# Sparse decode attention: sample by sample with positions on partitions, instead of all samples at once with heads on partitions

## What is computed

```python
_, sel = lax.top_k(sc, n_sel)                       # 256 of 2049 positions
rows_past = cache_kv[phys, pidx % PAGE_SIZE]        # keys and values, 2 kv heads x 64
s = jnp.einsum('bqcgd,bqncd->bqcgn', qg, k_sel).astype(jnp.float32) * DSA_SCALE
bias = rel_bias[t5_bucket(q_pos[None, :, None] - sel)]
s = jnp.where(valid[:, :, None, None, :], s + bias.astype(jnp.float32), -jnp.inf)
p = jax.nn.softmax(s, axis=-1)
o = jnp.einsum('bqcgn,bqncd->bqcgd', p, v_sel.astype(jnp.float32))
```

## Time and profile before

| | us |
|---|---|
| median of three runs (lowest, highest) | 1309.33 (1307.5, 1312.77) |
| the profiled execution | 1306.96 |
| its span, from the first instruction to the last | 1305.2 |
| TensorE busy in the span | 1190.2 (91%) |
| VectorE busy | 674.9 (52%) |
| ScalarE busy | 396.8 (30%) |
| GpSimd busy | 91.3 (7%) |
| end of the last `expand` (MLA decode) | 673.5 |
| first matmul of the output projection | 814.96 |

### The profile page before, as it was taken

The page is one execution under the profiler, slowest core; times in us unless marked ns, Lnnn a source line. Parts: engine busy times, 40 slices in busy tenths (PEclk is TensorE's granted clock), DMA queues, the critical chain, the costliest instruction groups (busy, mean ns, idle before and its releaser), DMA issues.

```text
span 1305.2 us, 22152 instructions
## 1 busy us (share of the span) xinstructions
PE 1190.2 (91%) x8993; PEld 1035.9 (79%) x8993; DVE 674.9 (52%) x1449; ACT 396.8 (30%) x766; POOL 91.3 (7%) x135
## 2 busy tenths in 40 slices
PE   6699999978999999999979966976999999979997
PEld 4588885444878999999865345966999999979997
DVE  1635835638897877777651031527333344276330
ACT  3322324523676555555542311012010100100001
POOL 2000002002035000001000010000000000000000
PEclk9799999979999999999987978987999999989999
DMA  9587631022011021113216634221333333332321
GB/s 324 151 268 196 191 114 41 3 70 90 2 74 74 1 74 74 74 74 138 76 65 219 241 141 197 72 58 33 97 88 88 96 89 88 86 89 75 99 72 65
DMA packets 138529, 135.96 MB, mean 104 GB/s; under 512 B 18222, under 2 KB 132283, under 8 KB 135668
## 3 DMA queue, kind: packets, MB, share of 16 engines
q1 hardware_dynamic: 133668, 83.29, 22.0%
q0 software_dynamic: 4784, 51.60, 10.4%
HBM read 131.40 MB, written 3.47 MB: 103 GB/s over the span
## 4 chain that ended last, share of the span: by engine, by line
PE 78%; DVE 11%; DMA 5%; ACT 3%; issue 2%; SPq 1%; POOL 0%; DVEq 0%; ACTq 0%
PE psV L1118 22%; PE psV L943 13%; PE psA L1118 10%; PE psA L686 6%; PE psV L1058 3%; PE psV L880 2%; PE psV L904 2%; PE psA L923 2%; PE psV L642 2%; DMA wide<-cache_kv,rows_of 2%; PE psA L1050 2%; PE psV L748 2%; PE psA L980 2%; PE psV L1089 1%; DVE wide_r L2062 1%
## 5 line engine op out<-in xcount | busy, mean ns | idle before, releaser
L943 PE MATMUL psV<-r_r,wide_r 128*128 128x260 f32 x1536 | 206.4, 288 | 3.6 <-DVE msk L1887 3.2
L943 PEld LDWEIGHTS psV<-r_r,wide_r 128*128 128x128 f32 x1536 | 190.1, 189 | 5.5 <-issue 2.9
L1118 PE MATMUL psV<-qiz_r,wring_r 128*128 128x260 f32 x688 | 124.0, 284 | 0.0
L1409 ACT ACTIVATE wring<-psV 128x512 f32<-128x512 f32 x128 | 76.3, 598 | 86.1 <-PE psV L943 69.7
L1118 PEld LDWEIGHTS psV<-qiz_r,wring_r 128*128 128x128 f32 x688 | 100.5, 190 | 0.0
L1888 DVE TENSOR_REDUCE msk<-wring 128x8 f32<-128x512 f32 x128 | 86.5, 676 | 0.0
L686 PE MATMUL psA<-wide_r,wring_r 128*128 128x260 f32 x432 | 79.7, 289 | 6.6 <-DVE hT_r L2097 6.6
L2051 DVE TENSOR_TENSOR wide<-wide,psV 128x520 f32 (+1 forms) x22 | 15.3, 696 | 134.7 <-PE psV L1118 134.7
L1118 PE MATMUL psA<-qiz_r,r_r 128*128 128x260 f32 x352 | 71.8, 286 | 14.1 <-DVE hT_r L2005 14.1
L1118 PE MATMUL psA<-hT_r,r_r 128*128 128x260 f32 x352 | 71.9, 286 | 0.0
L1118 PE MATMUL psA<-qiz_r,wring_r 128*128 128x260 f32 x352 | 71.4, 285 | 0.0
(11 more groups left out here) (464 smaller groups left out, 2483.3 us busy)
## 6 DMA issues: line engine op xcount, KB each, us to landing
wring<-w_ffn_in SPq DMA_DIRECT2D x44, 512.0 KB, 3.7
wide<-w_ada SPq DMA_DIRECT2D x11, 1024.0 KB, 6.9
wring<-w_ffn_out SPq DMA_DIRECT2D x16, 704.0 KB, 4.7
tok<-w_ada SPq DMA_DIRECT2D x9, 1024.0 KB, 8.1
wring<-w_in SPq DMA_DIRECT2D x24, 256.0 KB, 3.4
wring<-w_out SPq DMA_DIRECT2D x8, 512.0 KB, 4.4
wring<-w_in SPq DMA_DIRECT2D x20, 128.0 KB, 2.7
hT<-x_prompt SPq DMA_DIRECT2D x4, 512.0 KB
```

What stands on the lines that cost most here:

```text
L943: mm = pe.matmul(kx[m % 2][:, hf, :], w, wtab[:, b % 2, l, 2 * k + hf, :], start=(k == 0 and w is high and l == 0), stop=(k == 1 and w is ...
L1118: mm = pe.matmul(out[:, hf, 0:HT], w[:, k, :], x[:, hf * HT:(hf + 1) * HT], start=(k0 + k == 0 and x is xh and w is high), stop=(k0 + k == ...
L1409: A(sq2[m % 2].rearrange("p (x n) -> p x n", x=2), kx[m % 2][:, :, 0:256], ACT.Square).then_inc(kx_squared, 1)
```

## The change

The sparse decode is written like the MLA decode, with positions on partitions, one sample after the other. `k_product` now writes the scores of one sample (`dps`, 128 positions x 17 slots x 8 heads) with the transposed keys as weights and the sample's 8 queries as moving data. `sparse_scores` adds the bias and the mask (`bmd`), and `shift`, `exps`, `row_sums`, `normalise`, `head_max` and `head_sum` serve the sparse samples as b = 8 to 15. `weigh_values(b)` uses the value half of the same buffer, so each sample is fetched once. The mask stays on the chip (`maskx`); its HBM round trip, the 64-row softmax and its transposes, `qdz` and `ptb` are gone. The bias table `far` is made once, during the prompt attention (`far_table`), and `bmd` per sample by GpSimd (`mask_bias`), two samples ahead. The `latent_out` matmuls of group A are done sample by sample within the MLA decode. The first output weights are loaded when the mask is ready, and the prompt's part of the projection input is split apart from the samples' part (`split_prompt`). In part, with "..." where lines are left out:

```diff
+            def far_table():
...
+                for j in range(NPG + 1):
+                    cols = ohf[:, j:PAST:NPG] if j < NPG else ohf[:, PAST:PAST + 1].broadcast_to([NBUCK, 128])
+                    mm = pe.matmul(farps[:, j * 8:(j + 1) * 8], cols, rb64[:, 0:8], start=True, stop=True, skip_group_check=True)
+                mm.then_inc(far_full, 1)
...
+                if u == 8:
+                    far_table()
...
+                if j == 10 and b >= 1:
+                    pe.wait_ge(lat_out, b)
+                    mm = latent_out(b - 1)
...
+                for x in range(4):
+                    j = c4 * 4 + x
+                    mm = pe.matmul(dps[:, j * 8:(j + 1) * 8], kdT[:, c4 % 2, x * 128:(x + 1) * 128], qd[:, b * 8:(b + 1) * 8],
+                                   start=True, stop=True, skip_group_check=True)
...
+            def weigh_values(b):
+
+                pe.wait_ge(pm_ready, NB + b + 1)
+                pe.wait_ge(lat_out, NB + b)
+                for j in range(NPG + 1):
+                    rows = kvp[b % 3][:, j, 128:256] if j < NPG else tok[:, 4, 416:544]
+                    q = 32 * (j % 4)
+                    mm = pe.matmul(latd[q:q + 32], pm32[b % 2][:, j, :], rows, start=(j < 4), stop=(j > NPG - 4), skip_group_check=True)
+                mm.then_inc(lat_pv, 1)
...
+            for b in range(NB):
+                weigh_values(b)
+                if b >= 1:
+                    values_out(b - 1)
+                if b + 2 < NB:
+                    k_scores(b + 2)
...
+            for b in range(NB):
+                if b >= 1:
+                    exps(NB + b)
+                for c4 in range(4 if b + 1 < NB else 0):
+                    if b == 0 and c4 == 2:
+                        exps(NB)
+                    take_keys(4 * b + 4 + c4)
+                take(NB + b)
...
+            for b in range(NB):
+                sparse_scores(b)
+                for step in (shift, row_sums, normalise):
+                    step(NB + b)
...
+            def mask_bias(b):
+                if b == 0:
+                    g.wait_ge(far_taken, 1)
+                    g.wait_ge(mask_ready, 1)
+                if b >= 2:
+                    g.wait_ge(d_taken, b - 1)
+                g.tensor_tensor(bmd[:, b % 2].rearrange("p (j h) -> p j h", h=8), far,
+                                maskx[:, b, :].unsqueeze(2).broadcast_to([128, NPG + 1, 8]), ALU.add).then_inc(bm_ready, 1)
...
+                if b == NB - 3:
+                    for x in range(2):
+                        mask_bias(x)
...
-            for b in range(2, NB):
-                if b >= 3:
-                    g.wait_ge(a_full, A_KD + 4 * b - 8)
-                kv_rows_of(b, b % 3)
...
+            for b in range(NB):
+                head_max(NB + b)
+                if b + 2 < NB:
+                    g.wait_ge(lat_pv, NB + b)
+                    kv_rows_of(b + 2, (b + 2) % 3)
+                head_sum(NB + b)
+                if b + 2 < NB:
+                    mask_bias(b + 2)
```

More of the change, by code:

```diff
@@ L950, in expand, with latent_out @@
                     mm = pe.matmul(last_total[:, 8:16], earlier, ends[:, 8:16], start=True, stop=True, skip_group_check=True)
-                mm.then_inc(kx_full, 1)
+                elif m % 4 == 2 and KA + m // 4 == STEPS + 1:
+                    pe.wait_ge(top_done, 1)
+                    mm = pe.matmul(newm, maskx[:, :, NPG], ident[:, 127:128], start=True, stop=True, skip_group_check=True)
+                if j == 10 and b >= 1:
+                    pe.wait_ge(lat_out, b)
+                    mm = latent_out(b - 1)
+                mm.then_inc(kx_full, 1)
+            def latent_out(b):
+                for k in range(2):
+                    mm = pe.matmul(olps[:, k * 8:(k + 1) * 8], olr[b % 2][:, k * 128:(k + 1) * 128], sel[:, 64:72], start=True, stop=True,
+                                   skip_group_check=True)
+                return mm
             def rope_turn(b):
@@ new lines, in k_product, with k_scores @@
+                if c4 == 3:
+                    mm = pe.matmul(dps[0:NB, 128:136], kT[:, SEQ:T], qd[:, b * 8:(b + 1) * 8], start=True, stop=True, skip_group_check=True)
+                    mm.then_inc(d_full, 1)
+            def k_scores(b):
+                for c4 in range(5):
+                    if c4 < 4:
+                        k_turn(b, c4)
+                    if c4 >= 1:
+                        k_product(b, c4 - 1)
+            def weigh_values(b):
[6 more added lines that the diff above has]
+                mm.then_inc(lat_pv, 1)
@@ new lines, in values_out @@
+            def values_out(b):
+                pe.wait_ge(lat_out, NB + b + 1)
+                mm = pe.matmul(odps[:, b * 8:(b + 1) * 8], olr[b % 2][:, 0:128], sel[:, 64:72], start=True, stop=True, skip_group_check=True)
+                if b == NB - 1:
+                    mm.then_inc(od_full, 1)
+            k_scores(0)
+            weigh(NB - 1)
+            k_scores(1)
+            pe.wait_ge(lat_out, NB)
+            latent_out(NB - 1).then_inc(ol_full, 1)
+            for b in range(NB):
[5 more added lines that the diff above has]
+                if b == 0:
+                    pe.wait_ge(ol_taken, 1)
+                    pe.wait_ge(v_free, V_OV - 1)
+                    for h in range(H):
+                        for k in range(2):
+                            mm = pe.matmul(sv(V_OV)[(h % 2) * 64:(h % 2) * 64 + 64, 0, (h // 2) * 8:(h // 2) * 8 + 8],
+                                           wukv[:, k, h * 128 + 64:(h + 1) * 128], olT[:, k, :].rearrange("p (b h) -> p h b", b=NB)[:, h, :],
+                                           start=(k == 0), stop=(k == 1), skip_group_check=True)
+                    mm.then_inc(v_full, 1)
@@ L1100, in pe_tail @@
+            values_out(NB - 1)
         def pe_tail(pe):
```

270 lines of the change are left out of this document (91 added, 179 removed).

## The result

The changed kernel took 1359.1 us (median of 4 runs, 1342.21 to 1362.61) beside 1311.05 us for the kernel before on the same chip: ratio 1.0326, 95% interval 1.0228 to 1.0425. It is 48 us slower, where 28 was forecast. The time lies inside the range, the direction is right, and the mechanism in the sparse decode is the one that was named. But the largest part of the loss arises elsewhere, in the prompt attention. The ratio is one of means, and leaves out the longest run of the changed kernel (1362.61, counted as slow), which is the profiled one; so ratios are taken from the runs, and shares from the traces. Its span is 1360.5 us, 55.3 more than before.

A forecast was written before the change was run, and what follows sets the result against it. TensorE was taken to bound the kernel outside the sparse decode, GpSimd's switches the new sparse decode. There +21.4 us, with +6.4 from small terms before it: +27.8 on 1309.33 gives 1337 us, range 1300 to 1362.

The forecast's parts named there:

- The switches: Sparse decode: GpSimd passing from reduction to TENSOR_TENSOR and back, 10 and 8.5 us, a pair per sample, period 21.1 us.
- the +21.4 of the forecast: Sparse decode: the output projection would start at 836.4 us instead of 815.0, before the shift from earlier terms.
- The direction that had no row of its own: GpSimd's switch from TENSOR_TENSOR back to the reduction: bounded by 0 and 33 us, taken at 8.5.
- The slowing by a fetch: Sparse decode: the first switch of a pair runs beside a fetch, so it was taken at 10 us, not 8.5.
- Both rivals with cheap switches: GpSimd's switches at 6 us each, 1298 us, chance 0.11; or costing nothing that counts, 1256 us, chance 0.05.
- The free period of 8.4 us: Sparse decode without switch costs: 8.4 us per sample, set by the fetch; TensorE's own sum was 7.6.
- The rival with free switches: GpSimd's bare ISA rows cost nothing that counts: 8.4 us per sample, total 1256 us; chance 0.05.
- pairs of 21 to 24.6: Rival in the sparse decode: fetches slow GpSimd's switches still more, total 1355 to 1375 us; slower than forecast had chance 0.14.
- the signs that were named: Profile after: GpSimd gaps of 8 to 12 us, reductions 21 us apart, TensorE waits, clock 0.5 to 0.7, projection near 843.
- The far table: Prompt attention: `far_table` adds 34 TensorE instructions of 0.112 us, 3.8 us in all, bounds 2.7 and 7.6.
- `latent_out`: MLA decode: 28 added TensorE instructions, 3.1 us.
- The switches around `mask_bias(0)` and `(1)`: End of MLA decode: this GpSimd pair needs some 19 us and just fits; up to 4 us more if slowed.

The follow-up runs named there:

- e4: Changed kernel with the fetch of sample b + 2 issued by GpSimd behind mask_bias(b + 2), not between head_max and head_sum: 1351.79 us, one run.
- e1: Changed kernel with mask_bias issued by VectorE and no longer by GpSimd: 1309.41 us.
- e3: Kernel before plus 17 unread matmuls at attention step 8, weights 32 x 128 (every 16th column), 8 moving columns: 1339.31 us, ratio 1.0208.
- e7: Kernel before plus the burst of e3, but with 128 adjacent weight columns per matmul and not every 16th: 1332.77 us, ratio 1.0166.
- e2: Changed kernel with the far table's 17 matmuls issued one per attention step, 8 to 24, and copied at step 26, not 10: 1341.15 us.
- e5: Changed kernel with the edits of e1 and e2, and adjacent weight columns for the far table: 1292.11 us, ratio 0.9864.
- e9: Changed kernel with mask_bias on VectorE, and the far table in one burst with adjacent columns in the sparse decode: 1284.96 us, ratio 0.9817.

## Why the prediction was right, and where it was not

**The switches.** Right in place, cause and nearly in size. Forecast 18.5 us for a pair (10 and 8.5) and a period of 21.1; measured 9.8 to 11.2 plus 5.8 to 6.0, and 19.4. Five periods are 97.1 us where 105.5 were forecast, which is about the difference between the +21.4 of the forecast and the +13.2 measured there. The direction that had no row of its own, back to the reduction, was taken at 8.5 and is 5.9. The slowing by a fetch, taken at 1.5, is 3.5 to 4, on a base of 7.0 and not 8.5 (e4): that the sum of 10 came out near 10.8 is two errors that nearly cancel. e1 shows that the switches set the period: without them it is 12.96 us. Both rivals with cheap switches fall, since a pair is 16 to 17 us. The Trainium skill's figure, about 6 us (GPSIMD Engine Reference, section 2.1 Instruction dispatch), agrees with the direction to the reduction alone (5.9); the other took 6.8 at best.

**The free period of 8.4 us** was never tested by the changed kernel, and e1 shows it wrong as a rule: TensorE's own work is 13 us per sample at the low clock. The prediction used the low clock for the last sample alone; by its text TensorE works 8 us of each 21, and it was 13.4 of 19.4 (67.15 us in five periods). The figure itself was near where the clock was high: 9.05 us in e1 and 8.80 in e6. The rival with free switches would have come out near the 1309 of e1 and not at 1256 with the far table where it was.

**Luck in the total.** The forecast's own bracket, pairs of 16 to 21 us, was 1322 to 1352. The pair came out in it, and the time, 1359.1, lies above it, next to the 1355 to 1375 that was given to pairs of 21 to 24.6. So the time lies inside the range of 1300 to 1362 by 3 us, and through a loss for which the range was not drawn. Of the signs that were named, GpSimd's gaps ahead of TENSOR_TENSOR, the clock of 0.5 to 0.7 in the sparse decode and TensorE's wait of 6 us per sample came true. The reductions at 5.9 us in place of 8 to 12, the projection at 867 in place of 843, and the sparse decode shifted by 38.9 us (678.11 to 716.97) in place of 6.4 did not.

**The far table** is the step that failed: "`far_table` adds 34 instructions of 0.112 = 3.8 us to the prompt attention (bounds 2.7 and 7.6 ...)". The burst takes 7.5 us, at the upper bound, since columns spaced by 16 cost 0.22 us an instruction (e3 against e7). And from its middle on TensorE runs at half the clock for 58 us, another 28. The working of the prediction priced TensorE's instructions at the clock of the trace before, and never asked what the new ones would do to that clock, though it had a clock of 0.50 beside a busy TensorE in its own rows. The term measured +35.2 us in the trace. In the medians the miss of 20 us (48 less 28) comes out about so, by an estimate that adds the median of e3 to terms of single traces: e3, with the burst alone, is 28 slower, 24 more than the 3.8 of the forecast; the sparse decode cost 8.2 less, `latent_out` 0.6 more, the end 3.2 more.

The Trainium skill (TensorE: Matmul & The Clock Gate, section Why this matters for your kernels) asks for no idle gaps of TensorE between bursts if the clock is to hold. Here there was no gap: TensorE was busy for all of 343.50 to 350.20 and the clock fell. The rule doesn't cover this case, and the measurement decides.

**The small terms.** `latent_out`: forecast 3.1, measured 3.7 with all else from the first reduction to the last `head_max` of the MLA decode. The switches around `mask_bias(0)` and `(1)` fit, as forecast, with 0.4 us at most to show for them (e1, without them, has 33.35 us where this has 33.77): the `head_max` of sample 6 waited for VectorE at its end and came 33.8 us after the one before, where the earlier ones lie 32.1 to 33.8 apart. From the projection on nothing was to change; the profiled execution has +3.2. In the traces of e1, e2, e3, e4, e5 and e9 this stretch takes 489.1 to 493.7 us, with no pattern in the edits, so I put it to scatter, which isn't shown.
